# A hybrid decoder step: the first tile's output norm one page further on in the last cached sequence

## The reference

```python
z = rms_norm(x) @ w_in                       # q latent, kv latent, rotary key, conv input
# group A: conv = silu(layer_norm(causal_depthwise_conv(glu(u))))
# group B, attend_sample, for each page of each cached sequence:
k_nope, v = expand_kv(ckv, lp)               # ckv @ w_uk, rms_norm per head; ckv @ w_uv
sc = attn_scores(q_nope, q_pe, k_nope, kpe)  # two parts: latent and rotary
carry = online_update(carry, sc, v)          # softmax over pages and the own tokens
# both groups
mix = concatenate([rms_norm(attn), rms_norm(conv)])
x = x + mix @ w_out
x = x + (silu(h @ w_gate) * (h @ w_up)) @ w_down          # h = rms_norm(x)
x = x + sigmoid(rms_norm(x) @ w_ple_gate) * (pe @ w_ple_proj)
```

## Time and profile before

| what | us |
|---|---|
| median of 3 runs | 1690.11 |
| lowest and highest run | 1689.55, 1691.83 |
| the profiled execution's own time | 1691.84 |
| its span | 1689.9 |
| TensorE busy | 1649.4 (98%) |
| VectorE busy | 1239.2 (73%) |
| ScalarE busy | 658.5 (39%) |
| GpSimd busy | 528.4 (31%) |

### The profile page before, as it was taken

How to read it: one execution, slowest core, us unless ns; L and a number is a source line. 1 busy time by engine, 2 the same in 40 slices (tenths; PEclk the granted TensorE clock), 3 DMA queues, 4 the chain that set the end, 5 groups by cost and what they waited for, 6 DMA issues and landing times.

```text
span 1689.9 us, 29020 instructions
## 1 busy us (share of the span) xinstructions
PE 1649.4 (98%) x10698; PEld 1483.4 (88%) x10698; DVE 1239.2 (73%) x1851; ACT 658.5 (39%) x1240; POOL 528.4 (31%) x361
## 2 busy tenths in 40 slices
PE   8999999999999999999989999999999999999998
PEld 7999887776999989878879999999999888788886
DVE  5396887677899999876798777777776676954444
ACT  5302345764544444654442222222222335442111
POOL 2303696420656565531223222222221000600000
PEclk9999999999999999999999999999999999999999
DMA  5501000002252222230114444444444877662101
GB/s 179 164 1 49 15 1 1 2 2 55 56 164 59 59 59 64 82 107 1 51 50 150 146 145 145 144 146 145 145 146 152 293 262 245 196 221 70 46 31 47
DMA packets 156045, 172.89 MB, mean 102 GB/s; under 512 B 35155, under 2 KB 107376, under 8 KB 155805
## 3 DMA queue, kind: packets, MB, share of 16 engines
q1 hardware_dynamic: 153939, 170.52, 31.6%
q10 hardware_dynamic: 2002, 1.03, 0.2%
HBM read 131.06 MB, written 40.80 MB: 102 GB/s over the span
## 4 chain that ended last, share of the span: by engine, by line
PE 75%; DVE 13%; POOL 5%; issue 3%; ACT 2%; DMA 1%; SPq 1%; ACTq 0%; POOLq 0%; DVEq 0%
PE ps L2636 20%; PE ps L2638 20%; PE ps L2637 20%; POOL stats L986 3%; PE ps L2895 2%; DVE arena L2198 2%; PE ps L2868 1%; DVE dn_lo L2410 1%; PE ps L3073 1%; DVE arena L1800 1%; POOL arena L1029 1%; PE ps L2848 1%; PE ps L626 1%; PE ps L2958 1%; PE ps L2642 1%
## 5 line engine op out<-in xcount | busy, mean ns | idle before, releaser
L1136 POOL TENSOR_TENSOR arena<-arena,mhalf 128x32 f32<-128x32 f32 (+1 forms) x40 | 179.5, 4495 | 113.2 <-DVE arena L2203 113.2
L2636 PE MATMUL ps<-cw_hi,pT_hi 128*128 128x288 f32 x512 | 163.9, 320 | 1.0 <-POOL cw_lo L1095 1.0
L2410 DVE TENSOR_TENSOR dn_lo<-dn_raw,dn_hi 128x1024 fp32r<-128x1024 f32 x83 | 115.3, 1400 | 61.4 <-ACT dn_hi L1703 60.4
L1800 DVE SCALAR_TENSOR_TENSOR arena<-arena,tapw 128x1024 f32<-128x1024 f32 x120 | 158.5, 1321 | 1.9
L2636 PE MATMUL ps<-T_hi,S_hi 128*128 128x272 f32 x528 | 152.7, 289 | 3.6 <-DVE F_B_r L680 1.8
L2637 PE MATMUL ps<-F_B_r,S_hi 128*128 128x272 f32 x528 | 152.3, 288 | 0.0
L2638 PE MATMUL ps<-T_hi,S_lo 128*128 128x272 f32 x528 | 152.0, 288 | 0.0
L2637 PE MATMUL ps<-cw_lo,pT_hi 128*128 128x288 f32 x512 | 150.8, 294 | 0.0
L2638 PE MATMUL ps<-cw_hi,pT_lo 128*128 128x288 f32 x512 | 150.7, 294 | 0.0
L1703 ACT ACTIVATE dn_hi<-dn_raw 128x1024 fp32r<-128x1024 f32 x83 | 87.5, 1059 | 132.3 <-DMA dn_raw<-wt_mid 62.4
L2636 PE MATMUL ps<-dn_hi 128*128 128x512 f32 x308 | 120.5, 391 | 0.8 <-DVE dn_lo L2410 0.6
(11 more groups left out here) (407 smaller groups left out, 4864.6 us busy)
## 6 DMA issues: line engine op xcount, KB each, us to landing
dn_raw<-act_mid SPq DMA_DIRECT2D x77, 256.0 KB, 2.9
arena<-in_cache_ckv SPq DMA_DIRECT2D x128, 128.0 KB, 2.1
dn_raw<-in_w_down SPq DMA_DIRECT2D x45, 256.0 KB, 3.7
w_raw<-in_w_gate SPq DMA_DIRECT2D x22, 512.0 KB, 4.0
w_raw<-in_w_up SPq DMA_DIRECT2D x22, 512.0 KB, 5.3
arena<-in_w_down SPq DMA_DIRECT2D x22, 512.0 KB, 5.9
act_mid<-arena SPq DMA_DIRECT2D x11, 1024.0 KB, 7.7
wt_mid<-arena SPq DMA_DIRECT2D x11, 1024.0 KB, 4.4
```

What stands on the lines that cost most here:

```text
L1136: nc.gpsimd.tensor_tensor(rstd_k[:, g0:g1, :], ms_k[:, g0:g1, :], mhalf[:, 0:(g1 - g0) * NH].rearrange("p (g h) -> p g h", h=NH), ALU.pow) ...
L1800: ins = nc.vector.scalar_tensor_tensor(y_of(c), glu[:, c, k:k + SEQ], tapw[:, c, k:k + 1], y_of(c), ALU.mult, ALU.add)
L2410: nc.vector.tensor_tensor(dn_lo_r[s], dn_raw[s], dn_hi[s][0], ALU.subtract).then_inc(s_("a_split"), 1)
L2636: mm(out, left[0], right[0], start=start, stop=False)
```

## The change

All of it is in the last cached sequence (`b == NSEQ - 1`) and right behind it.

- `centre(0)` goes from page 5 to page 6, where it stands behind `shift`; `variance(0)` from 6 to 7; `layer_norm(0)` from 7 to 8; `mix_stat(0)` from 9 to 10; `mix_scale(0)` from 10 to 12. In a page they now stand ahead of the low split of a weight.
- On ScalarE `centred_square(0)` goes from page 6 to 7 and `conv_silu(0)` from 8 to 9.
- On GpSimd `ln_pool(1)`, which stood behind the first power of page statistics, now stands behind the second, with `mix_pool(1)`.
- The splits of weight blocks 7 and 2 go from page 9 to pages 10 and 11.
- The transpose of the last rotary keys goes to bank K0 + 1, at the columns that K0 + 3 has for the others. It now waits for the evacuation of page 14 (`ksq_ready`), which frees that bank, and not for `sc_used`.

```diff
-WO_PAGE = dict(zip(WO_ORDER, (3, 4, 8, 9, 9, 13, 14)))
+WO_PAGE = dict(zip(WO_ORDER, (3, 4, 8, 10, 11, 13, 14)))
...
-            return K0 + 3 if 4 * b + q < 4 * NSEQ - 1 else PE_BANK
+            return K0 + 3 if 4 * b + q < 4 * NSEQ - 1 else K0 + 1
...
-                    if b == NSEQ - 1 and q == 0:
+                    if b == NSEQ - 1 and q == 1:
                         ln_pool(1, P)
-                    if b == NSEQ - 1 and q == 1:
                         mix_pool(1, P)
...
-                        if g == 6:
+                        if g == 7:
                             centred_square(0)
-                        if g == 8:
+                        if g == 9:
                             conv_silu(0)
...
                     if b == NSEQ - 1:
+                        if g == 6:
+                            centre(0)
+                        if g == 7:
+                            variance(0)
+                        if g == 8:
+                            layer_norm(0)
+                        if g == 10:
+                            mix_stat(0)
+                        if g == 12:
+                            mix_scale(0)
                         for k in (k for k in WO_PAGE if WO_PAGE[k] == g):
                             low_wo(k)
-                        if g == 5:
-                            centre(0)
-                        if g == 6:
-                            variance(0)
-                        if g == 7:
-                            layer_norm(0)
-                        if g == 9:
-                            mix_stat(0)
-                        if g == 10:
-                            mix_scale(0)
...
-            pe.wait_ge(s_("sc_used"), 4 * NSEQ - 1)
+            pe.wait_ge(s_("ksq_ready"), NPAGE * NSEQ - 1)
             kpe_T(NSEQ - 1, 3)
             kpe_scores(NSEQ - 1, 3)
```

## The result

The changed kernel takes 1696.09 us (median of 22 runs, 1692.39 to 1698.86) against 1693.37 us for the kernel before (median of 22 runs beside them, 1688.94 to 1696.97). The ratio is 1.0016 with a 95% interval of 1.0008 to 1.0023, so the change costs 2.7 us, with an interval of some 1.4 to 3.9. The forecast was +3.1 us. In absolute terms the forecast of 1693.2 and its upper end, 1694.6, lie under the measured time: the three runs that were shown first are among the 22, and their median of 1690.11 is 3.3 us under that of all.

What follows compares the result with a forecast made beforehand. VectorE, the full queue behind page 7, was taken to set TensorE's end through the maxima. Held at the layer norm, it delivers them 3.1 us later: 1691.84 becomes 1694.9, less 1.7 to the median gives 1693.2 us, range 1690.9 to 1694.6.

Steps and rivals of the forecast that it cites:

- Edit 1: VectorE, centre behind the shift: shift 1.29 us sooner, TensorE's wait before page 9 shrinks from 1.83 to 0.5 us.
- Edit 2: GpSimd order, ln_pool(1) behind the large power: VectorE stands 3.9 to 4.2 us at the layer norm, which starts at 712.50.
- rival (b): Layer norm isn't held, GpSimd's power ending sooner; mix_scale in page 12 puts all 0.8 us later: 1690.9 us. Chance 0.09.
- Edits 3 and 4: VectorE, moved splits and mix steps: same cost elsewhere in the queue; low_m at 729.6, 3.1 us later.
- The table load: ScalarE at page 9: Silu's load hides in the wait for the layer norm and costs nothing; uncovered, 1.28 us.
- rival (a): ScalarE's conv_silu(0) at page 9: table load runs only after the wait, 1.3 us more, 4.4 in all: 1694.5. Chance 0.12.
- Edit 5: TensorE's rope transposes in K0 + 1: two waits become one; 0.5 us gained becomes a wait before max_T, worth nothing.
- Rival (d): The key bank for the last rope transposes gives its 0.5 us after all: 1692.7 us. Chance 0.08.
- The sum: VectorE's last maxima come 3.1 us later, at about 738.0, and TensorE carries this to the end: +3.1 us.
- The base: Profiled execution, 1691.84 us, lies 1.7 above the shown runs' median of 1690.11; forecast 1694.9 becomes 1693.2.
- The chances: Whole kernel against a bound of 0.2%, 3.4 us: slower 0.37, faster 0.04, within 0.2% 0.59.

Runs made afterwards that it cites:

- e9: Kernel before with only the norm's steps one page later, small power first, splits and rope bank as before: 1693.43 us, ratio 0.9993.
- e2: Changed kernel with ln_pool(1) put back ahead of the large power on GpSimd, so without the hold: 1694.01 us, ratio 1.0007.
- e3: Kernel before with only ln_pool(1) put behind the second power, so the hold alone: 1699.66 us, ratio 1.0040.
- e10: Changed kernel with the splits of weight blocks 7 and 2 put back to page 9: 1696.59 us, ratio 1.0019.
- e11: Kernel before with only the splits of weight blocks 7 and 2 moved to pages 10 and 11: 1698.51 us, ratio 1.0032.
- e1: The changed kernel once more, with no edit: 1697.0 us, ratio 1.0024.
- e4: Kernel before with only the last rope transposes moved to bank K0 + 1: 1694.53 us, ratio 1.0000.
- e7: e6 with the rope bank of e4 in addition: 1692.99 us, ratio 0.9999.
- e6: Kernel before with the norm early: centre at page 0, its square at 2, variance at 3, layer norm at 6: 1692.74 us, ratio 0.9995.
- e5: Changed kernel with 15 filler products between the last rope transpose and its scores: 1698.3 us, ratio 1.0027.
- e12: e7 with splits drawn together in pages 7 to 9 and the steps behind the norm one page later: 1691.28 us, ratio 0.9990.
- e13: e12 with the last split, of block 4, at page 13 and not 14: 1690.97 us, ratio 0.9987.

## Why the prediction was right, and where it was wrong

**Edit 1, right.** The wait before page 9 went from 1.83 to 0.6 (forecast 0.5), and e9 shows the norm's move alone as a gain of 0.7 us, about half of the 1.3 by which the shift is sooner.

**Edit 2, right, and it is the cause.** Forecast a hold of 3.9 to 4.2 us at the layer norm, measured 4.20; forecast layer norm at 712.50, measured 714.48 - 1.64 = 712.84. The third of a us is the 0.46 between the end of the small power (714.02) and the layer norm's start, for which the sum had no term. That the span of the large power is to be believed (5.54 us, its successor 5.51 behind it) decided against rival (b). Taking the hold out (e2) takes 2.5 of the 3.25 us off the maxima; putting it in puts 5.2 on them alone (e3) and 4.2 behind the moved norm (e10 against e9).

**Edits 3 and 4, right in the sum, wrong as said.** low_m was forecast at 729.6 and came at 729.78; page 14 forecast near 722.4, came at 724.28 - 1.64 = 722.64; page 12's wait forecast 0.9, measured 0.99. But the sentence "they have the same cost elsewhere in the queue" is true only behind the hold (e10, where undoing them changes 0.2 us). Alone they cost some 2 us even with the first fall taken off (e11), and without the hold 1.4 (e2 against e9). I had taken VectorE's work as a sum of durations, and had not asked which pause each split stood in. That the sum held with this sentence in it was in part luck: it holds for this order of the queue and not for its parts. Rival (b), the change without a hold, was put at +0.8, and e2 has +0.7 at the maxima, but not for (b)'s reason: mix_scale is in its new page in e9 too, which gains.

**The table load, right.** It ran from 711.37 to 712.65 and was over 3.3 us before its activation started, inside ScalarE's wait; rival (a) fell.

**Edit 5, right.** One wait for quad 2, 2.04 us (forecast about 2), and its gain turns up as a wait before max_T, 0.42 in e1 and 0.44 in e4. e7 against e6, in another order, is the same to 0.02 us of stretch. Rival (d) fell, as far as 0.1% can tell.

**The sum, right as a difference:** +3.1 forecast, +2.7 measured in 22 runs (interval 1.4 to 3.9), +3.3 in e1's stretch. The last maxima are 3.25 later.

**The base, wrong.** The step that failed is the base under the sum, "it lies 1.7 above the median of the runs shown, 1690.11": the 1.7 us were taken off as if that median were the kernel's, and it measured 1693.37 in 22 runs. It was of three runs, and this kernel's executions spread over 8 us, as 22 runs show (1688.94 to 1696.97). The sum was put on a point near the low end of that spread, and the range of -2.3 and +1.4 around it held only errors of the sum. On the median of the 22 the same sum gives 1693.37 + 3.1 = 1696.5, 0.4 over what was measured. The sentence "as much in the medians" gave 0.6 us to an error that was 3.3. Three runs this low are bad luck too: of all triples of the 22, 7% have a median of 1690.11 or less. The median also moves between sets of runs, 1693.74, 1693.61, 1691.62 and 1693.38 in the four sets run beside the experiments.

**The spread itself, a term that was missing.** It goes with falls of TensorE's clock, which come at a handful of places outside the stretch (about 9, 27, 205 to 220, 225, 290 and 860 us): at 9 us in all 14 traces, at each of the others in some and not in others. Over the 116 runs of before beside the experiments, the 21 with a mean granted clock of 0.997 took 1689.2 to 1693.4 us, the 15 with 0.993 or less 1695.0 to 1698.9. Three windows of the execution of before, then the same of after:

```profile
288.00:298.00 10.00, 10.00 (x68) 8.24 (x67) 4.69 (x9) 6.60 (x17) 1.07 (x1) 1.00 0.00 0
686.00:760.00 74.00, 69.50 (x466) 58.75 (x464) 57.59 (x117) 44.72 (x92) 31.86 (x15) 1.00 0.29 92
860.00:868.00 8.00, 7.85 (x60) 7.44 (x60) 7.83 (x12) 6.39 (x8) 0.00 (x0) 1.00 0.01 2
```

```profile
288.00:298.00 10.00, 10.00 (x41) 7.37 (x41) 2.74 (x6) 4.63 (x11) 0.32 (x1) 0.66 0.00 0
686.00:760.00 74.00, 66.77 (x446) 56.10 (x446) 56.87 (x115) 42.93 (x89) 33.92 (x14) 0.98 0.29 93
860.00:868.00 8.00, 6.15 (x38) 5.89 (x38) 7.04 (x13) 4.27 (x8) 0.54 (x1) 0.79 0.01 2
```

At 288 and 860 us both kernels do the same work, and only after's execution ran it at a lower clock: 10 x 0.34 = 3.4 us and 8 x 0.21 = 1.7 us of clock time. (The first is the lateness of 1.64 us at the stretch's start, less what before had lost at other places.) Summed over the whole span, (1 - granted clock) by its windows is 5.7 us in before's execution and 10.7 in after's. Before the result I had read the clock of the stretch as 1.00 and stopped there. A fall belongs in a forecast in two ways: as spread of the base, and as a price of a new wait. Seven kernels have falls in the stretch (after, e2, e3, e4, e5, e10, e11), and each begins within some two us of the end of a wait of TensorE of 1.4 us or more; the four whose longest wait there is 1.1 or less (e6, e7, e12, e13) have none. A wait isn't needed everywhere: in after's trace the waits of TensorE have no entry from 280 to 289 us, and the clock falls at 289. How likely a given wait brings one is open: 2.04 us did in after and not in e1; 1.83 did in e4 and e11 and not in before or e3.

**The chances.** 0.59 for "within 0.2%", 0.37 for slower. The measured ratio, 0.16%, is within 0.2%, and its interval excludes no change at all: with 22 runs on each side a smaller difference can be told than the 0.2% I had set.

## What to carry to other kernels

An instruction that is moved behind another on a queue inherits its whole length: 0.54 us of power put behind 5.54 us of power cost 2.5 to 4.2 us at the maxima, more than everything else in the change, on an engine that is busy for 31% of the span. Before a step is called free to move, look for the pause that it fills (its neighbours' releasers), not only at the queue's sum. And before a forecast of a few tenths of a per cent is put on an absolute time, ask what the spread of the base is: three runs of this kernel gave its median to no better than 3 us.

## What the runs showed of the hardware

- TensorE's granted clock falls to 1.2 GHz behind some of its idle times of about 2 us and not behind others of the same length in the same program (2.04 us in after and in e1), and at 289 us of after with no wait in the 9 us ahead. One fall loses 1.5 to 1.7 us, and executions of one kernel differ by 8 us. The Trainium skill (TensorE: Matmul & The Clock Gate, What's actually happening) says that the hardware's watch on the engine's activity isn't tied to the kernel's start, so that the same kernel differs from run to run. The two traces agree with that.
- GpSimd's power (TENSOR_TENSOR, pow) took 0.54 us for 128x1, 0.71 for 128x2, and 5.54 for 128x32 (6.40 once, at 698.29 of after). So it matters much which of two goes first. Some 0.46 us passed between its end (714.02) and the start of the instruction waiting (714.48).
- A table load of ScalarE ran ahead of its activation's wait once more (711.37, its activation at 715.99), 1.28 us. Where its activation followed at once (before, 708.83 to 710.13) no drain is to be seen between them.
